# Grouped-key attention on one core: values issued four steps behind their scores in place of three

## The chip, the cores and the metric

One core of one Trainium2 chip runs the whole program. The metric is the device time of one execution in microseconds (us); of several executions the median is given. The engines are named as in the profile: PE (matmul), PEld (its weight loads), DVE (vector), ACT (scalar), POOL (GpSimd) and SP (which only issues DMAs here). Each runs its own instructions in order and waits for the others on semaphores.

## What is computed

The program chains a first block (pool mixer, windowed attention, feed-forward with convolution) and a second block of two attention layers, with 1024 tokens and 256 context tokens of width 1024, all in float32. The change lies in the first of the two layers, where 16 query heads of width 64 share 4 key heads:

```
def gqa_attend(q, k, v):
    s = jnp.einsum('bqhgd,bkhd->bhgqk', q, k).astype(jnp.float32) * (GQA_HEAD_DIM ** -0.5)
    p = jax.nn.softmax(s, axis=-1).astype(v.dtype)
    return jnp.einsum('bhgqk,bkhd->bqhgd', p, v)
...
    k_all = jnp.concatenate([kc, k], axis=1)
    v_all = jnp.concatenate([vc, v], axis=1)
    o = sweep_query_blocks(lambda qb: gqa_attend(qb, k_all, v_all), q).reshape(B, S, GQA_WIDTH)
    y = (o * jax.nn.silu(g)) @ p["w_out"]
...
        oc = gqa_attend(qc, kc, vc).reshape(B, L, GQA_WIDTH)
```

The 1024 tokens attend to all 1280 keys; the 256 context tokens attend to the 256 context keys. The second layer (called mla in the code) uses the same class of the kernel with other sizes.

## The kernel before, in words

The class `Attention` runs one attention layer for all 16 heads. The 1280 queries stand in three chunks (`CHUNKS_ALL`: 512, 512 and the 256 of the context), the keys in tiles of 128. A **step** is one key tile against one chunk: ten for each of the first two chunks, two for the context chunk, 22 a head. Two heads (44 steps, `self.SB`) make one turn of an 8-turn loop, in which the steps of one turn and the last values of the turn before are laid into each other. Operands are split into a high and a low part in a reduced float32 form so that products keep their precision.

What a step k does, engine by engine:

- PE, `scores` (L2253, L2254): two matmuls into one of two PSUM banks (`self.S[k % 2]`). It waits until exp of step k-2 has read the bank.
- ACT, `probs`: exp from PSUM into `gqa_pf` (L2314), then a copy into the reduced form, the high half `gqa_ph` (L2320). There are four buffers each of `PF`, `PH` and `PL`; exp of k waits for the low part of k-4, the high half of k waits for the values of k-4. Between the two ACT instructions, at certain steps, stand the two ACT instructions of the reciprocal (`rden`, L2330, L2332: a logarithm of the row of denominators, then exp of its negative).
- POOL, in some steps DVE (`low`, L2366): the low part `gqa_pl` = pf - ph. DVE takes it in steps 7, 9, 13 and 19 of a head (`dve_lo`), one step later in its own order.
- PE, `values` (L2268 to L2270): three matmuls that add into the output bank of the chunk. It waits for the low part. The output of the context chunk is kept in the bank `BC`.

Beside these, the row maxima of a later head or chunk are prepared. The table `self.plan` says at which step of a head PE passes over the keys (`maxima`, L2223, into the one PSUM area `PMX`: steps 0, 2 and 4 for chunk 1, step 6 for the context chunk, 10, 12, 14 and 16 for chunk 0 of the next head, 18 for its chunk 1); DVE reduces it (L2388), and after the last pass of a chunk DVE builds a diagonal matrix (L2396); in steps 8, 11 and 20 PE spreads it over the partitions (`bcast`, L2234, into `BC`), and ACT copies one row into the query tile (`row`, L2307). A pass of maxima waits for the reduction of the pass before. A broadcast waits for the diagonal, for the row before it, and for the multiply by the reciprocal (`self.norm`) of all chunks of the heads before, since that reads `BC`.

When a chunk has its last values, ACT makes the reciprocal and DVE runs `final`: a multiply of the output with the reciprocal into `gqa_t` (L2407, signals `norm`), and a multiply with the gate into `MIX` (L2412).

The order of the instructions of every engine is fixed when the program is built. In its step k, PE issues maxima and broadcasts of step k, then `scores(k)`, then `values(k - LAG)`. ACT runs the reciprocal of a chunk `LAG + 1` steps behind the chunk's last step (context chunk: `LAG + 2`). DVE issues the reductions and diagonals of step k, the low part of step k-1 where it is its own, and then the `final` that is due, by `self.lags`:

```
self.lags = (self.LAG + 4, self.LAG + 4, 0) if self.mla else (self.LAG + 5, self.LAG + 2, self.LAG + 3)
...
self.run(pe, first_steps, lambda i, k: values(i, k - self.LAG), self.LAG)
...
lags, lag = (self.LAG + 1, self.LAG + 1, self.LAG + 2), self.LAG + (1 if self.mla else 2)
```

The last steps of the chunks are 9, 19 and 21 of a head.

Of the kernel before, what the change touches and what calls it, by code (L numbers as in the profile page):

```python
# [104 lines left out]
def mixed_program(nc, A, out):  # L105

    ctx = ExitStack()
    with ctx:

        def sem(name):  # L110
            return ctx.enter_context(nc.semaphore(name))
# [4 lines left out]
        class Scope:  # L116


            def __init__(self):
                self.stack = ExitStack()  # L120
# [1880 lines left out]
        def head_buffers(name, scope, q, layout, nq, side="left"):  # L2001

            return ([scope.sb(f"{name}_k{a}{q}", [P, N], R32, side) for a in range(2)],
                    [scope.sb(f"{name}_q{a}{q}", [P, nq], R32, side) for a in range(2)],
                    [scope.sb(f"{name}_v{a}{q}", [P, N // P, P], R32, side) for a in range(2)])
# [5 lines left out]
        class Attention:  # L2011
# [4 lines left out]

            LAG = 3

            def __init__(self, name, scope, chunks, keys, scale, layout, mix, first, first_maxima):
                self.name, self.chunks, self.keys, self.scale, self.mix = name, chunks, keys, scale, mix
                self.mla = layout == "mla"
                self.row = 96 if self.mla else 64

                self.K, self.Q, self.V = zip(first, head_buffers(name, scope, 1, layout, chunks[-1][0] + chunks[-1][1]))
                self.G = scope.sb(f"{name}_gate", [P, chunks[-1][0] + chunks[-1][1]])
                self.PF = [scope.sb(f"{name}_pf{b}", [P, C]) for b in range(4)]
                self.PH = [scope.sb(f"{name}_ph{b}", [P, C], R32) for b in range(4)]
                self.PL = [scope.sb(f"{name}_pl{b}", [P, C], R32) for b in range(4)]  # L2030
                self.D = [first_maxima[0], scope.sb(f"{name}_d1", [P, 4, P], R32)]
                self.M = first_maxima[1]
                self.dim = 96 if self.mla else 64
                self.nq = chunks[-1][0] + chunks[-1][1]
                self.load_inc = 16 * (4 if self.mla else 6)

                self.const_n = 32 + 3 + (32 if self.mla else 0)
                self.v_and_const = [sem(f"{name}_v_and_const{q}") for q in range(2)]
                self.RD = scope.sb(f"{name}_rd", [64, C])
                self.T = scope.sb(f"{name}_t", [P, C])  # L2040
                self.loaded = [sem(f"{name}_loaded{q}") for q in range(2)]
                self.gate_loaded = sem(f"{name}_gate_loaded")
                (self.max, self.red, self.diag, self.bcast, self.row_done, self.scores, self.exp, self.hi,
                 self.lo_pool, self.lo_dve, self.pv, self.rden, self.norm, self.fin) = [sem(f"{name}_{x}") for x in (
                     "max", "red", "diag", "bcast", "row", "scores", "exp", "hi", "lo_pool", "lo_dve", "pv",
                     "rden", "norm", "fin")]
                self.S = [PB[0], PB[1]]
                self.BC = PB[2]
                self.FREE = self.BC if self.mla else PMX[:, 0:C]
                self.O = [PD[0], PD[1], self.BC]  # L2050

                self.steps = [(q, c, t, x == 0, x == len(keys[c]) - 1) for q in range(2) for c in range(len(chunks))
                              for x, t in enumerate(keys[c])]
                self.SB = len(self.steps)
                self.NC = len(chunks)

                if self.mla:
                    plan = [(2 * t, "max", (0, 1), t) for t in range(4)] + [(8, "bcast", (0, 1), 0)]  # L2060
                    plan += [(10 + 2 * t, "max", (1, 0), t) for t in range(4)] + [(18, "bcast", (1, 0), 0)]
                    self.ahead = [(0, t) for t in range(4)]
                else:
                    plan = [(2 * t - 2, "max", (0, 1), t) for t in range(1, 4)] + [(6, "max", (0, 2), 0)]
                    plan += [(8, "bcast", (0, 1), 0), (11, "bcast", (0, 2), 0)]
                    plan += [(10 + 2 * t, "max", (1, 0), t) for t in range(4)]
                    plan += [(18, "max", (1, 1), 0), (20, "bcast", (1, 0), 0)]
                    self.ahead = [(0, t) for t in range(4)] + [(1, 0)]
                self.plan = plan
                self.NT = sum(1 for p in plan if p[1] == "max")  # L2070
                self.fin_all = HEADS * self.NC + CR_FIN2
                self.norm_all = HEADS * self.NC + CR_N

                self.dve_lo = lambda k: k % (self.SB // 2) in ((3, 8, 13, 18) if self.mla else (7, 9, 13, 19))
                self.lags = (self.LAG + 4, self.LAG + 4, 0) if self.mla else (self.LAG + 5, self.LAG + 2, self.LAG + 3)
                self.n_dve = sum(1 for k in range(self.SB) if self.dve_lo(k))
                self.n_pool = self.SB - self.n_dve
# [123 lines left out]
            def pe_begin(self, pe):  # L2201
# [25 lines left out]
                def bcast(i, c, g):  # L2227
                    n = self.chunks[c][1]
                    pe.wait_ge(self.diag, i * (2 * NC) + (g + 1))

                    pe.wait_ge(self.row_done, i * (2 * NC) + (g + CR_ROW2))
                    if NC == 3:
                        pe.wait_ge(self.norm, i * (2 * NC) + ((g - 1) // NC * NC + CR_N))
                    pe.matmul(self.BC[:, 0:n], ones[:, :], self.D[g % 2][:, 0:n // P, :], start=True, stop=True)\  # L2234
                      .then_inc(self.bcast, 1)
# [21 lines left out]
                def values(i, k):  # L2257
                    q, c, t, first, last_ = self.steps[k]
                    n = self.chunks[c][1]
                    self.wait_lo(pe, i, k)  # L2260
                    if first and c == 0:
                        pe.wait_ge(self.v_and_const[q], i * 32 + self.const_n)
                    if first:

                        pe.wait_ge(self.norm, i * (2 * NC) + (q * NC + c - NC + CR_N + 1))
                    o = self.O[c][:, 0:n]
                    ph, pl = self.PH[k % 4][:, 0:n], self.PL[k % 4][:, 0:n]
                    pe.matmul(o, self.V[q][0][:, t, :], ph, start=first, stop=False)  # L2268
                    pe.matmul(o, self.V[q][1][:, t, :], ph, start=False, stop=False)  # L2269
                    pe.matmul(o, self.V[q][0][:, t, :], pl, start=False, stop=last_).then_inc(self.pv, 1)  # L2270
# [4 lines left out]
                def step(i, k, last):  # L2275
                    for kind, q, c, t, g, tile, over in self.tasks(k, last):
                        if kind == "max":
                            maxima(i, q, c, t, tile, c == 0 and t == 0, i + 1 if over else i)
                        else:
                            bcast(i, c, g)  # L2280
                    scores(i, k)

                def rest(bank_free):
                    def first_steps(i, k, last):
                        if isinstance(i, int) and i == 0 and k < 2:
                            bank_free(k)
                        step(i, k, last)
                    self.run(pe, first_steps, lambda i, k: values(i, k - self.LAG), self.LAG)
                return ahead, lambda: bcast(0, 0, 0), rest
# [7 lines left out]
            def act_begin(self, act):  # L2297
# [41 lines left out]

                lags, lag = (self.LAG + 1, self.LAG + 1, self.LAG + 2), self.LAG + (1 if self.mla else 2)  # L2340

# [1213 lines left out]
```

## Time and profile before

| what | us |
| --- | --- |
| median of 3 runs | 3461.96 (3459.22 to 3461.97) |
| the profiled execution | 3465.23 |
| its span, first to last instruction | 3463.3 |
| busy in the span: PE, DVE, ACT, POOL | 3330.5, 2261.4, 1769.3, 1538.4 |

The profile is of one execution. A start and a duration are in us from the start of the span. A duration of a matmul includes the time in the pipeline, so that consecutive matmuls overlap: two matmuls of 512 columns start 0.23 us apart and are shown with 0.39 us each. What a matmul costs is therefore read from start to start. PE appears as busy for nearly the whole program, in this stage too.

### The profile page before, as it was taken

How to read it: one execution, taken by the hardware profiler on the slowest of the kernel's cores; microseconds unless marked ns; L12 is line 12 of the kernel's file. 1: busy time of each engine (PE TensorE's matmuls, PEld its weight loads, DVE VectorE, ACT ScalarE, POOL GpSimd, SP SyncE). 2: the span in 40 equal slices, each digit the busy share in tenths (PEclk: the TensorE clock that was granted, in tenths of full speed). 3: DMA queues.
4: the chain of work that ended last, by engine and by line, in shares of the span. 5: the costliest groups of instructions: out<-in, count | busy, mean ns of one | idle time of the engine just before them, and what ended most of it. 6: DMA issues, size and time to landing. Idle time of an engine off the chain costs nothing.

```text
span 3463.3 us, 47931 instructions
## 1 busy us (share of the span) xinstructions
PE 3330.5 (96%) x14993; PEld 2652.2 (77%) x14993; DVE 2261.4 (65%) x2647; ACT 1769.3 (51%) x3039; POOL 1538.4 (44%) x962
## 2 busy tenths in 40 slices
PE   7999999999999999999999999999998989999999
PEld 5778878778888888778777777778765668888877
DVE  6674878677576665638537777777558875555551
ACT  3343878332010101334339999971455558888880
POOL 3403444544444445410037777767220026666662
PEclk9999999999999999999999999999999999999999
DMA  2134232411213121123344434413255344232312
GB/s 103 49 115 136 55 86 52 154 53 55 85 47 99 49 85 58 61 70 118 117 116 99 96 82 95 106 49 109 100 198 157 124 120 129 58 81 67 70 36 80
DMA packets 196088, 313.56 MB, mean 91 GB/s; under 512 B 100928, under 2 KB 111680, under 8 KB 195968
## 3 DMA queue, kind: packets, MB, share of 16 engines
q1 hardware_dynamic: 195968, 312.01, 31.3%
q8 instruction: 70, 1.15, 0.1%
q14 instruction: 50, 0.41, 0.0%
HBM read 234.02 MB, written 77.92 MB: 90 GB/s over the span
## 4 chain that ended last, share of the span: by engine, by line
PE 66%; POOL 10%; issue 9%; DVE 9%; ACT 4%; DMA 1%; SPq 0%; POOLq 0%; DVEq 0%; ACTq 0%
PE PBX L283 11%; PE PBX L285 10%; PE PBX L284 10%; POOL gqa_pl L2366 8%; PE PMX L283 4%; PE PMX L284 4%; PE PMX L285 4%; PE PMX L2223 2%; PE PD L2268 2%; PE PD L2269 2%; PE PD L2270 2%; PE PBX L2250 2%; PE PBX L2249 2%; PE PBX L2251 2%; PE PD L1013 2%
## 5 line engine op out<-in xcount | busy, mean ns | idle before, releaser
L216 POOL TENSOR_TENSOR w_hi<-w_stage,zero 128x1024 fp32r<-128x1024 f32 (+2 forms) x116 | 223.6, 1927 | 1173.6 <-PE PBX L285 875.7
L2366 POOL TENSOR_TENSOR gqa_pl<-gqa_pf,gqa_ph 128x512 fp32r<-128x512 f32 (+1 forms) x288 | 381.6, 1342 | 146.8 <-ACT gqa_ph L2320 145.0
L2366 POOL TENSOR_TENSOR mla_pl<-mla_pf,mla_ph 128x512 fp32r<-128x512 f32 x256 | 341.9, 1341 | 207.8 <-ACT mla_ph L2320 202.3
L2388 DVE TENSOR_REDUCE mla_m<-PMX 128x1 f32<-128x1280 f32 x128 | 190.9, 1491 | 173.2 <-PE PMX L2223 173.0
L2388 DVE TENSOR_REDUCE gqa_m<-PMX 128x1 f32<-128x1280 f32 x144 | 201.6, 1400 | 150.5 <-PE PMX L2223 149.8
L218 POOL TENSOR_TENSOR w_lo<-w_stage,w_hi 128x1024 fp32r<-128x1024 f32 (+2 forms) x116 | 293.9, 2534 | 9.1
L1904 ACT ACTIVATE conv_in<-PBX 128x512 f32<-128x512 f32 x66 | 39.4, 599 | 478.9 <-PE PBX L285 474.9
L2314 ACT ACTIVATE mla_pf<-PBX 128x512 f32<-128x512 f32 x320 | 190.1, 594 | 82.1 <-PE PBX L2251 67.8
L2320 ACT ACTIVATE gqa_ph<-gqa_pf 128x512 fp32r<-128x512 f32 (+1 forms) x352 | 214.9, 611 | 12.4 <-PE PD L2270 0.4
L2314 ACT ACTIVATE gqa_pf<-PBX 128x512 f32<-128x512 f32 (+1 forms) x352 | 200.6, 570 | 31.0 <-PE PBX L2254 20.1
L283 PE MATMUL PBX<-ffn_hi,w_hi 128*128 128x512 f32 x528 | 207.2, 392 | 4.5 <-DVE ffn_lo L710 4.5
L2320 ACT ACTIVATE mla_ph<-mla_pf 128x512 fp32r<-128x512 f32 x320 | 201.8, 631 | 11.4
L285 PE MATMUL PBX<-ffn_hi,w_lo 128*128 128x512 f32 x528 | 206.2, 390 | 0.0
L284 PE MATMUL PBX<-ffn_lo,w_hi 128*128 128x512 f32 x528 | 206.1, 390 | 0.0
L1933 DVE SCALAR_TENSOR_TENSOR conv_out<-conv_in,VEC,conv_out 128x1024 f32<-128x1024 f32 x88 | 188.0, 2136 | 12.8 <-DVE conv_out L1933 0.6
L283 PE MATMUL PBX<-l_hi,w_hi 128*128 128x512 f32 (+1 forms) x400 | 158.6, 396 | 8.1 <-DVE l_lo L710 6.2
L478 DVE SCALAR_TENSOR_TENSOR PMX<-mod_w,cond_s 128x1024 f32<-128x1024 f32 x96 | 159.6, 1663 | 5.7 <-DVE PMX L478 0.6
L1929 DVE TENSOR_SCALAR conv_out<-conv_in,VEC 128x1024 f32<-128x1024 f32 x44 | 73.1, 1662 | 134.5 <-ACT conv_in L1904 133.8
L1620 POOL TENSOR_TENSOR swa_pl<-swa_pf,swa_ph 128x512 fp32r<-128x512 f32 x64 | 81.5, 1273 | 157.4 <-ACT swa_ph L1545 157.1
L2268 PE MATMUL PD<-gqa_ph,gqa_v 128*128 128x512 f32 x320 | 138.2, 432 | 7.9 <-POOL gqa_pl L2366 4.6
L285 PE MATMUL PBX<-l_hi,w_lo 128*128 128x512 f32 (+1 forms) x400 | 145.0, 362 | 0.0
L284 PE MATMUL PBX<-l_lo,w_hi 128*128 128x512 f32 (+1 forms) x400 | 144.7, 362 | 0.0
(526 smaller groups left out, 9961.5 us busy)
## 6 DMA issues: line engine op xcount, KB each, us to landing
mod_w<-in_w_mod SPq DMA_DIRECT2D x48, 512.0 KB, 3.5
w_stage<-in_w_up SPq DMA_DIRECT2D x44, 512.0 KB, 3.5
w_stage<-in_w_go SPq DMA_DIRECT2D x24, 512.0 KB, 3.7
gqa_k<-kh_d SPq DMA_DIRECT2D x32, 320.0 KB, 5.1
gqa_q<-qh_d SPq DMA_DIRECT2D x32, 320.0 KB, 6.8
w_stage<-in_w_down SPq DMA_DIRECT2D x24, 384.0 KB, 3.1
qh_d<-heads_qh SPq DMA_DIRECT2D x32, 256.0 KB, 2.0
ql_d<-heads_ql SPq DMA_DIRECT2D x32, 256.0 KB, 2.3
```

What stands on the lines that cost most here:

```text
L216: pool.tensor_tensor(w_hi[s][:, 0:st.cols], w_stage[s][:, 0:st.cols], z, ALU.add).then_inc(w_hi_done, 1)
L218: pool.tensor_tensor(w_lo[s][:, 0:st.cols], w_stage[s][:, 0:st.cols], w_hi[s][:, 0:st.cols].bitcast(F32), ALU.subtract).then_inc(w_split, 1)
L283: pe.matmul(ps, wh, xh, start=first, stop=False)
L284: pe.matmul(ps, wh, xl, start=False, stop=False)
L285: return pe.matmul(ps, wl, xh, start=False, stop=last)
L478: dve.scalar_tensor_tensor(out=PMX[:, C:3 * C], in0=bufs[s], scalar=1.0, in1=conds[j], op0=ALU.mult, op1=ALU.mult, accum_out=MOD[:, bass.d ...
L1933: dve.scalar_tensor_tensor(out=y, in0=CU[s][:, j:j + S], scalar=w(j), in1=y, op0=ALU.mult, op1=ALU.add).then_inc(conv_step, 1)
L2268: pe.matmul(o, self.V[q][0][:, t, :], ph, start=first, stop=False)
L2314: act.activation(self.PF[k % 4][:, 0:n], self.S[k % 2][:, 0:n], ACT.Exp, scale=self.scale)\
L2320: act.activation(self.PH[k % 4][:, 0:n], self.PF[k % 4][:, 0:n], ACT.Copy).then_inc(self.hi, 1)
L2366: eng.tensor_tensor(self.PL[k % 4][:, 0:n], self.PF[k % 4][:, 0:n], self.PH[k % 4][:, 0:n].bitcast(F32), ALU.subtract).then_inc(self.lo_dv ...
L2388: dve.tensor_reduce(self.M[g % 2][:, t:t + n], PMX[:, 0:n * w].rearrange("p (n w) -> p n w", n=n), AX.X, ALU.max, negate=True).then_inc(se ...
```

## The change

The constant `LAG` of the class, 3, becomes a value of each object: 3 for the mla layer, 4 for the grouped-key layer. Everything that is counted from it follows: `values` of step k stand behind `scores` of step k+4; the reciprocals of the chunks move from steps 13, 1 and 4 to 14, 2 and 5; the finals on DVE from 17, 2 and 5 to 18, 3 and 6 (the later numbers of chunks 1 and 2 are steps of the next head). The number of buffers (four), the plan of the maxima, the steps whose low part DVE makes, and the number of instructions are the same. The unrolled start of the loop of each engine is one step longer.

```
-            LAG = 3
...
                 self.dim = 96 if self.mla else 64
+
+                self.LAG = 3 if self.mla else 4
```

## Rows read from the trace of the kernel before

**Rows 1.** Stretches: busy us (instructions) of each engine, granted clock, DMA share, GB/s

```profile
1786.00:2303.00 517.00, 504.54 (x2206) 388.70 (x2206) 382.98 (x346) 469.71 (x846) 383.57 (x290) 1.00 0.41 86
...
1916.53:1948.55 32.02, 31.56 (x142) 24.45 (x141) 24.24 (x22) 29.37 (x53) 24.06 (x19) 1.00 0.47 102
1948.55:1980.60 32.05, 31.60 (x142) 24.43 (x141) 24.77 (x22) 29.39 (x53) 23.86 (x19) 1.00 0.40 82
```

**Rows 2.** Timeline of PE, a middle head: start us, us, line, tiles

```profile
1927.97 0.39 PE L2253 MATMUL PBX<-gqa_q,gqa_k 128*128 128x512 f32 x1
...
1948.55 0.40 PE L2253 MATMUL PBX<-gqa_q,gqa_k 128*128 128x512 f32 x1
...
1949.71 0.40 PE L2253 MATMUL PBX<-gqa_q,gqa_k 128*128 128x512 f32 x1
```

**Rows 3.** Page, chain that ended last: shares of the span by line

```profile
PE PBX L283 11%; PE PBX L285 10%; PE PBX L284 10%; POOL gqa_pl L2366 8%; PE PMX L283 4%; PE PMX L284 4%; PE PMX L285 4%; PE PMX L2223 2%; PE PD L2268 2%; PE PD L2269 2%; PE PD L2270 2%; PE PBX L2250 2%; PE PBX L2249 2%; PE PBX L2251 2%; PE PD L1013 2%
```

**Rows 4.** Waits from 1832.35 to 2280.6: waiter <- awaited, us, times, longest

```profile
PEld PD L2268 <- POOL gqa_pl L2366: 37.2, 91, 0.7
...
ACT gqa_pf L2314 <- PE PBX L2254: 13.4, 26, 1.0
...
ACT gqa_ph L2320 <- PE PD L2270: 0.4, 1, 0.4
```

**Rows 5.** Timeline of PE, steps 5 to 8 of a head

```profile
1955.34 0.39 PE L2254 MATMUL PBX<-gqa_q,gqa_k 65*128 65x512 f32 x1
1955.99 0.50 PE L2268 MATMUL PD<-gqa_ph,gqa_v 128*128 128x512 f32 x1 [0.26 <-POOL gqa_pl L2366]
1956.32 0.39 PE L2269 MATMUL PD<-gqa_ph,gqa_v 128*128 128x512 f32 x1
...
1956.79 0.39 PE L2223 MATMUL PMX<-gqa_k,gqa_q 128*128 128x256 f32 x2
...
1959.74 0.39 PE L2234 MATMUL PBX<-gqa_d,ones 128*128 128x512 f32 x1
```

**Rows 6.** Timeline of ACT, steps 0 and 1 of the same head

```profile
1949.29 0.60 ACT L2314 ACTIVATE gqa_pf<-PBX 128x512 f32<-128x512 f32 x1 [1.03 <-PE PBX L2254]
...
1951.08 0.60 ACT L2330 ACTIVATE gqa_rd<-PD 64x512 f32<-64x512 f32 x1
1951.71 0.63 ACT L2332 ACTIVATE gqa_rd<-gqa_rd 64x512 f32<-64x512 f32 x1
```

**Rows 7.** Timeline of POOL, the same head

```profile
1952.94 8.82 POOL L2366 TENSOR_TENSOR gqa_pl<-gqa_pf,gqa_ph 128x512 fp32r<-128x512 f32 x6 [1.02 <-ACT gqa_ph L2320]
```

**Rows 8.** Timeline of DVE, steps 2 to 6 of the same head

```profile
1952.72 0.68 DVE L2407 TENSOR_TENSOR gqa_t<-PD,gqa_rd 64x512 f32<-64x512 f32 x1
1953.54 1.24 DVE L2412 TENSOR_TENSOR MIX<-gqa_t,gqa_gate 64x512 f32 x1
1954.71 1.47 DVE L2388 TENSOR_REDUCE gqa_m<-PMX 128x1 f32<-128x1280 f32 x1
1956.22 1.52 DVE L2396 TENSOR_TENSOR gqa_d<-ident_f,gqa_m 128x512 fp32r<-128x512 f32 x1
1957.66 0.41 DVE L2407 TENSOR_TENSOR gqa_t<-PBX,gqa_rd 64x256 f32<-64x256 f32 x1
...
1959.09 0.67 DVE L2388 TENSOR_REDUCE gqa_m<-PMX 128x2 f32<-128x512 f32 x1
1959.80 0.81 DVE L2396 TENSOR_TENSOR gqa_d<-ident_f,gqa_m 128x256 fp32r<-128x256 f32 x1
```

**Rows 9.** Timeline of DVE, the first head

```profile
1791.68 0.99 DVE L2396 TENSOR_TENSOR gqa_d<-ident_f,gqa_m 128x512 fp32r<-128x512 f32 x1
```

**Rows 10.** Timeline of PE, first head and last head

```profile
1801.06 0.85 PE L2223 MATMUL PMX<-gqa_k,gqa_q 128*128 128x512 f32 x3 [3.50 <-DMA gqa_v<-vl_d]
...
2280.07 0.40 PE L2234 MATMUL PBX<-gqa_d,ones 128*128 128x512 f32 x1
```

**Rows 11.** Timeline of ACT, last head, the row copy of step 8

```profile
2281.39 0.59 ACT L2307 ACTIVATE gqa_q<-PBX 1x512 fp32r<-1x512 f32 x1
```

## What the change is predicted to do, before it ran

> **What bounds the kernel now.** I read the stage windows first. The grouped-key stage runs from about 1786 to 2302 us, 517 us of the 3463.3 us span, at a full granted clock [rows 1]; the stage with the other layout keeps its lag of three and everything outside the stage issues the same instructions, so only these 517 us can change. Inside it one head of 22 steps repeats: two heads in a row took 32.02 and 32.05 us, with PE busy 31.6, ACT 29.4, DVE 24.2 to 24.8 and POOL 24.0 [rows 1]. PE looks full, but the page says a busy PE need not be at its peak, so I went by start-to-start times. Write S(k) for the two score matmuls of step k, V(k) for the three value matmuls, M for a maxima pass, B for a broadcast. A step without M lasts 1.16 us from S to S [rows 2]: five matmuls at 0.233. So S is 0.47, V 0.70, M 0.57 to 0.58, the small M of step 6 0.23, B 0.23, and a step of the context chunk (256 queries) 0.24 and 0.35.
>
> The chain that ended last gives POOL's low parts 8% of the span [rows 3], and the waits of the middle of the stage put 37.2 us on value matmuls that wait for POOL [rows 4]. That counts from the end of a weight load, so it overstates. By start-to-start times six V in a head start late: V(2) starts 0.65 us after its step's second score matmul in place of 0.235, and its own second matmul follows after 0.33 in place of 0.235, a loss of 0.51 us [rows 5]. The other five lose 0.41, 0.31, 0.31, 0.29 and 0.25 by the same reading; together 2.1 us a head. Without them PE's head is 32.0 - 2.1 = 29.9 us. The prize is at most 16 x 2.1 = 34 us.
>
> **The edits.** Every count is the same: no instruction, DMA or buffer is added. Three things move by one step.
>
> (a) V(k) is issued after S(k+4), not S(k+3). A high half follows its S by about 1.4 us, by 2.6 where a reciprocal (two ACT ops; its first begins 0.61 after its exp, its second 0.63 later [rows 6]) lies between; then the low part takes 1.29 to 1.47 (8.82 us for six [rows 7]). The late V above are those where this exceeds three steps. A further step gives 1.16 to 1.74 us, over twice the largest delay. I take all six delays as gone: -2.1 us a head. The lower bound is 0 (POOL is at 24.0 of 32, so it is no bound by itself).
>
> (b) ACT's high half of k needs V(k-4) out of the buffer. Before, V(k-4) was issued ahead of S(k); now it is behind it. S(k) starts at 0, exp(k) at 0.74 (S(0) at 1948.55, exp at 1949.29 [rows 2, 6]) and the high half would start at 1.37; V(k-4) starts at 0.47, its last matmul ends 0.87 later, about 0.1 goes to the hand-over, so 1.44. Cost: 0.07 us where ACT follows PE at once, nothing where it lags. ACT's own pair is 1.15 us and PE's step 1.16, so the 0.07 is paid once as an offset, not per step. Between 0 and 20 x 0.07 = 1.4 us a head; I take 0.
>
> (c) The ends of chunks. The reciprocals move from steps 13, 1 and 4 to 14, 2 and 5, and DVE's two multiplies of a chunk ("final") from 17, 2 and 5 to 18, 3 and 6. DVE executes in order, a step's maxima first, then its final. So the final of chunk 1 used to stand behind the reduction of step 2, and now stands alone in step 3, in front of the reduction of step 4; the final of the context chunk used to stand in front of step 6's reduction and diagonal, and now stands behind both. Two PE instructions wait for this: M of step 6 needs the reduction of step 4 (one PSUM area), and B of step 8 needs the multiply of the context chunk's final (it reads the bank that B writes). Before, B(8) came at 1959.74 and that multiply began at 1957.66 and took 0.41: 1.67 us of slack [rows 5, 8]. M(6) at 1956.79 came 0.6 after the reduction of step 4 (1954.71 + 1.47) [rows 5, 8].
>
> The new order, in us from S(0), by those durations: S(0) 0, V(18) 0.47, S(1) 1.16, V(19) 1.63, M(2) 2.33, S(2) 2.90, exp(2) 3.64 (ACT is free by 3.15). Reciprocal 4.25 and 4.88, done 5.51. Final of chunk 1 begins at 5.55. Then DVE runs without a gap, start to start as in [rows 8]: multiply 0.82, MIX multiply 1.17, reduction of step 4 1.51, diagonal 1.44, small reduction 0.71, small diagonal 0.75 to 0.81, then the context multiply 0.41: it ends at 12.36. M(6) can start at 9.1, where PE arrives at about 7.7; B(8) starts at 12.4, where PE could be at 10.1 by its own work. So 2.3 us of waiting per head stands in place of 1.2 us of late V ahead of B(8) before. After B(8): restart 0.34 (as at 1955.99 to 1956.32 [rows 5]), then S(8) to the next S(0). Before this was 1948.55 - 1927.97 = 20.58 us with 0.91 of late V in it, so 19.67 pure (the two starts are in [rows 2]). The head becomes 12.41 + 0.34 + 19.67 = 32.4 us, against 32.03. I followed ACT and POOL through these 20 us: exp(k-2) is out 0.3 us or more ahead of S(k), and the tightest low part (17) ends 0.5 us before its V.
>
> The other half of the heads shows the same DVE order; with the shorter ops that the trace also has for the same work (diagonal 0.99 in the first head [rows 9]) the chain is 0.3 shorter to 0.3 longer: head 32.1 to 32.75.
>
> The Trainium skill bears here, "SBUF — State Buffer", section "SBUF: two separate sides": it says that a VectorE op with two SBUF inputs and a GpSimd op that reads SBUF take a shared port pair as an exclusive lock, and that whoever comes second blocks for the other's whole instruction. This trace shows a milder thing: POOL's ops went from 1.29 to 1.47 and the diagonal next to them took 1.52 against 0.99 [rows 7 to 9]. By the rule at its full size the three ops of the new chain with two SBUF inputs could each wait out a POOL op of 1.29 us, 3.9 us a head in place of the 0.7 that the rows hold; it would end at the second rival or above.
>
> **The sum.** First head: PE waits for the second head's values from DRAM until 1801.06 whatever came before [rows 10]; its last two late V go, -0.6. Then 14 head to head periods at +0.38: +5.3. B(8) of the last head sits 12.41 - 11.19 = +1.2 later from its S(0). Behind it no maxima are left and ACT sets the pace; its row copy came 1.32 us after B(8) (2281.39 - 2280.07 [rows 10, 11]) and now can follow after 0.5: -0.85. Sum -0.6 + 5.3 + 1.2 - 0.85 = +5.1 us. The profiled execution took 3465.23 (span 3463.3), 3.3 above the median 3461.96; the sum gives 3470.3 for such an execution and 3467.1 for the median. With the heads at 32.1 to 32.75 this case spans 3463 to 3472.
>
> **Rivals.**
> 1. Faster: the final chain is short or begins early enough that M(6) and B(8) do not wait. Then only ACT's pace is left: exp(3), exp(6) and the like hold S by some 0.7 us a head, 29.9 + 0.7 = 30.6, so 14 x -1.4 - 0.6 - 0.85 = -21: 3441. For it: the late V are real and 34 us are there. Against: M(2) holds exp(2), and the seven DVE ops are counted in rows. It would need B(8) by 10.6, 1.8 us less than counted. Chance 0.13.
> 2. Slower by more: MIX, diagonal and small diagonal each wait out part of a POOL op that now stands elsewhere. By half of 1.29 us for each of the three, 1.9 us, less the 0.7 already in the rows taken: +1.2 a head, 14 x 1.2 + 5.1 = +22: 3484. It decides once the context multiply ends after 12.9 us from S(0). For it: POOL is busy without a break from low(2) on. Against: it was so in the rows I used. Chance 0.13.
> 3. No change: ACT, at 29.4 of 32 us, sets the pace under (b), loses what V gains, and the period stays within 0.1 us: 3462. Speaks for it: 92% busy. Speaks against: ACT waited 13.4 us for scores in the middle stretch, and only 0.4 for values [rows 4]. Chance 0.12.
>
> **Chances.** Forecast 0.62, rivals 0.13, 0.13, 0.12. A measurement of this kernel can tell some 0.2%, 6.9 us, from no change. Of the forecast's case about 0.4 of the width lies above +6.9 in view of errors of 0.1 us in each of seven ops, and a little below zero: slower 0.25 + 0.13 = 0.38; faster 0.13; same 0.37 + 0.12 = 0.49. The range leaves out most of rival 1 and half of rival 2: 3453 to 3480; the likeliest case's own is 3460 to 3474.
>
> **What would show it.** In the changed trace: (a) right if no value matmul waits for POOL in a middle head; (b) right if the high half waits for values by 0.1 us or less; (c) right if DVE runs seven ops without a gap between 5.5 and 12.4 us from S(0), if M(6) starts 0.05 to 0.1 after the reduction of step 4, and B(8) right behind the multiply of the context chunk, with PE gaps of about 1.4 and 0.8 us ahead of them, and S(0) to S(0) at 32.4. It is wrong if B(8) starts ahead of 11 us from S(0), if the reciprocal of chunk 1 runs at another step, or if POOL still holds values.

## The result and the profile after

The change made the kernel slower: 3473.56 us (median of 6 runs, 3471.29 to 3476.04) against 3461.26 (6 runs, 3459.22 to 3464.47), a ratio of 1.0032 with a 95% interval of 1.0021 to 1.0042. Measured once more in another series it was 1.004 (1.0027 to 1.0052). Forecast was 3467.1 with a range of 3453 to 3480: the sign of the forecast's sum (+5.1 us) and the mechanism came out, but the size was under half of the 12.3 us measured. The profiled execution has a span of 3474.1 us, 10.8 above that before.

The chain that ended last, from the page of the changed kernel, answers to [rows 3]: POOL's low parts, 8% before, are no longer among its listed lines, and POOL's part of the whole chain fell from 10% to 1%, while DVE's rose from 9% to 11%. First the shares by engine before the change, then those after it by engine and by line:

```profile
PE 66%; POOL 10%; issue 9%; DVE 9%; ACT 4%; DMA 1%; SPq 0%; POOLq 0%; DVEq 0%; ACTq 0%
...
PE 76%; DVE 11%; issue 6%; ACT 4%; POOL 1%; DMA 1%; SPq 0%; DVEq 0%; ACTq 0%; POOLq 0%
PE PBX L283 11%; PE PBX L285 10%; PE PBX L284 10%; PE PMX L283 4%; PE PMX L284 4%; PE PMX L285 4%; PE PMX L2224 4%; PE PD L2269 4%; PE PD L2270 4%; PE PD L2271 4%; PE PBX L2251 2%; PE PBX L2250 2%; PE PBX L2252 2%; PE PD L1013 2%; PE PBX L2255 2%
```

The waits of the changed kernel in the middle of the stage (1832.35 to 2290) answer to [rows 4]; columns: waiter <- awaited, us in all, times, longest.

```profile
PEld PMX L2224 <- DVE gqa_m L2389: 24.5, 14, 1.8
PEld PBX L2235 <- DVE gqa_t L2408: 9.7, 11, 0.9
PEld PBX L2254 <- ACT gqa_pf L2315: 6.8, 14, 0.5
...
ACT gqa_ph L2321 <- PE PD L2271: 0.9, 2, 0.7
...
DVE gqa_t L2408 <- ACT gqa_rd L2333: 13.9, 14, 1.1
```

(All lines of the class are one further down than before.) No value matmul waits for POOL. In place of the 37.2 us of [rows 4] PE waits for two things of DVE, once a head each: the small maxima pass of step 6 for a reduction, and the broadcast of step 8 for the context chunk's multiply. The last line is where the DVE chain starts: DVE stands idle there until the reciprocal is ready.

The timeline of DVE in one middle head, from the pass of step 2 to the low part of step 7 (S(0) of this head starts at 1949.65), answers to [rows 8]:

```profile
1952.78 1.49 DVE L2389 TENSOR_REDUCE gqa_m<-PMX 128x1 f32<-128x1280 f32 x1 [1.44 <-PE PMX L2224]
1955.32 0.68 DVE L2408 TENSOR_TENSOR gqa_t<-PD,gqa_rd 64x512 f32<-64x512 f32 x1 [1.05 <-ACT gqa_rd L2333]
1956.15 1.47 DVE L2413 TENSOR_TENSOR MIX<-gqa_t,gqa_gate 64x512 f32 x1
1957.56 1.47 DVE L2389 TENSOR_REDUCE gqa_m<-PMX 128x1 f32<-128x1280 f32 x1
1959.06 1.49 DVE L2397 TENSOR_TENSOR gqa_d<-ident_f,gqa_m 128x512 fp32r<-128x512 f32 x1
1960.47 0.68 DVE L2389 TENSOR_REDUCE gqa_m<-PMX 128x2 f32<-128x512 f32 x1
1961.19 0.80 DVE L2397 TENSOR_TENSOR gqa_d<-ident_f,gqa_m 128x256 fp32r<-128x256 f32 x1
1961.91 0.41 DVE L2408 TENSOR_TENSOR gqa_t<-PBX,gqa_rd 64x256 f32<-64x256 f32 x1
```

and the timeline of PE in the same head answers to [rows 2, 5]:

```profile
1949.65 0.40 PE L2254 MATMUL PBX<-gqa_q,gqa_k 128*128 128x512 f32 x1
...
1959.08 0.50 PE L2224 MATMUL PMX<-gqa_k,gqa_q 128*128 128x256 f32 x2 [1.25 <-DVE gqa_m L2389]
...
1962.37 0.50 PE L2235 MATMUL PBX<-gqa_d,ones 128*128 128x512 f32 x1 [0.44 <-DVE gqa_t L2408]
1962.70 0.39 PE L2254 MATMUL PBX<-gqa_q,gqa_k 128*128 128x512 f32 x1
...
1982.47 0.40 PE L2254 MATMUL PBX<-gqa_q,gqa_k 128*128 128x512 f32 x1
```

The reader is to see that DVE runs seven ops without a gap from 1955.32 to 1962.32, that PE's small pass starts 0.05 us after the reduction (1957.56 + 1.47 = 1959.03), that the broadcast starts 0.05 us after the multiply (1961.91 + 0.41 = 1962.32), and that a head lasts 1982.47 - 1949.65 = 32.82 us. Taken from the small pass of one head to that of the next, alternate heads of the changed kernel take 32.7 and 32.9 us; before they took 32.0 and 32.1. One head, from 2188.89 on, took 33.49. In it the granted clock of PE fell to half, 1.2 GHz in place of 2.4, right after PE's usual wait for the small pass, and the matmuls start 0.43 us apart in place of 0.23:

```profile
2189.00:2193.00 4.00, 4.00 (x12) 3.21 (x13) 3.36 (x5) 2.41 (x5) 2.90 (x3) 0.57 0.94 140
```

The third number from the end is the granted clock. PE had waited as long in the other heads without such a fall; why it came here isn't shown.

### The profile page after: what moved, and what is told of

It reads as the page before. It is cut to its first block, busy times and chain, and to the rows that moved or that the text cites. A ratio compares the mean times of both kernels' runs of the same rounds, so it can differ in the third digit from the quotient of the medians.

```text
span 3474.1 us, 47931 instructions
## 1 busy us (share of the span) xinstructions
PE 3320.1 (96%) x14993; PEld 2654.2 (76%) x14993; DVE 2256.6 (65%) x2647; ACT 1771.0 (51%) x3039; POOL 1539.6 (44%) x962
## 3 DMA queue, kind: packets, MB, share of 16 engines
q8 instruction: 70, 1.15, 0.1%
## 4 chain that ended last, share of the span: by engine, by line
PE 76%; DVE 11%; issue 6%; ACT 4%; POOL 1%; DMA 1%; SPq 0%; DVEq 0%; ACTq 0%; POOLq 0%
PE PBX L283 11%; PE PBX L285 10%; PE PBX L284 10%; PE PMX L283 4%; PE PMX L284 4%; PE PMX L285 4%; PE PMX L2224 4%; PE PD L2269 4%; PE PD L2270 4%; PE PD L2271 4%; PE PBX L2251 2%; PE PBX L2250 2%; PE PBX L2252 2%; PE PD L1013 2%; PE PBX L2255 2%
## 5 line engine op out<-in xcount | busy, mean ns | idle before, releaser
L283 PE MATMUL PBX<-h_hi,w_hi 128*128 128x512 f32 x336 | 138.8, 413 | 2.1 <-issue 1.1
```

Of the source, the lines that this page charges most:

```text
L283: pe.matmul(ps, wh, xh, start=first, stop=False)
```

## The experiments

All start from the changed kernel; a number after `else` is for the grouped-key layer. "Head" is the mean time from the small maxima pass of one head to that of the next, over 13 to 15 heads of the profiled execution. A head with a stretch at half clock is left out (one in the change, one with the reciprocals late). Waits "in the middle of the stage" are those from 1832.35 to 2270, which is 20 us less than in the list above; the change itself has 22.8 us for the small pass and 9.7 for the broadcast in it.

**Values four behind, ends where they were.**

```
-self.lags = ... else (self.LAG + 5, self.LAG + 2, self.LAG + 3)
+self.lags = ... else (8, 5, 6)
...
-lags, lag = (self.LAG + 1, self.LAG + 1, self.LAG + 2), self.LAG + (1 if self.mla else 2)
+lags, lag = (4, 4, 5), (4 if self.mla else 5)
```

> Only the values move to four steps behind; reciprocals stay at steps 13, 1 and 4 of a head and finals on DVE at 17, 2 and 5, as before the change. Theory (the chain of finals on DVE costs the time): the chain starts 1 us earlier and the context chunk's multiply stands ahead of the small reduction, B(8) waits for nothing, M(6) for about 0.6 us. Head 30.7 us from S(0) to S(0) against 32.0 before and 32.8 after; some 20 us faster than before, 3441. Rival (the coupling of the high half to the values, part b, costs the time): as slow as the change, 3473.

Measured: 3444.0 us, 0.9943 (0.993 to 0.9955) of before; head 30.64 us. The waits of PE in the middle of the stage (counted, as in [rows 4], from the end of a weight load):

```profile
PEld PBX L2254 <- ACT gqa_pf L2315: 6.0, 20, 0.7
PEld PMX L2224 <- DVE gqa_m L2389: 5.6, 14, 0.5
PEld PD L2269 <- POOL gqa_pl L2367: 1.8, 6, 0.3
```

The wait for POOL fell from 35.6 us before the change (37.2 up to 2280.6 [rows 4]) to 1.8 and nothing of that size came in its place. Moving the values alone is worth -1.4 us a head, so the loss of the change lies wholly in its other half, the ends. The rival that the coupling of the high half costs the time has fallen for a lag of four.

**Values three behind, ends as in the change.**

```
-self.LAG = 3 if self.mla else 4
+self.LAG = 3
...
-self.lags = ... else (self.LAG + 5, self.LAG + 2, self.LAG + 3)
+self.lags = ... else (9, 6, 7)
...
-lags, lag = (self.LAG + 1, self.LAG + 1, self.LAG + 2), self.LAG + (1 if self.mla else 2)
+lags, lag = ((4, 4, 5) if self.mla else (5, 5, 6)), (4 if self.mla else 6)
```

> Values stay three steps behind; reciprocals and finals move to the places they have in the change (14, 2, 5 and 18, 3, 6). Theory: B(8) at 12.7 us from S(0) as in the change, and the late values after B(8), 0.9 us a head, are still there: head 33.7, 14 x 1.65 = +23 us on before, 3484. Rival (values and high half): as before, 3461.

Measured: 3489.04 us, 1.0075 (1.0061 to 1.0088); head 33.77 us. Both kinds of wait stand side by side:

```profile
PEld PD L2269 <- POOL gqa_pl L2367: 25.6, 52, 1.3
PEld PMX L2224 <- DVE gqa_m L2389: 19.3, 13, 1.5
PEld PBX L2235 <- DVE gqa_t L2408: 10.8, 12, 0.9
```

So the parts don't add from the kernel before: the ends alone cost +1.75 us a head, the values alone bring -1.4, together they give +0.8 and not +0.35. Late values ahead of B(8) are hidden under the wait at B(8); taking them away there brings nothing once that wait exists. What the values still bring is 33.77 - 32.82 = 0.95 us a head, close to the 0.91 us of late values that the prediction had counted behind B(8).

**Which of the two ends: finals late, or reciprocals late.** Two kernels, each the change with one of them put back.

```
-lags, lag = (self.LAG + 1, self.LAG + 1, self.LAG + 2), self.LAG + (1 if self.mla else 2)
+lags, lag = (4, 4, 5), (4 if self.mla else 5)
```

> The change with its reciprocals back at 13, 1 and 4; finals on DVE stay at 18, 3 and 6. Theory: the multiply of chunk 1 can begin at 4.65 us from S(0), right behind the reduction of step 2, in place of 5.67; the rest of the DVE chain is the same, 7.1 us, so B(8) at 11.8 and a head of 31.9 us: 3460, 13 us below the change. Rival: as the change, 3473.

```
-self.lags = ... else (self.LAG + 5, self.LAG + 2, self.LAG + 3)
+self.lags = ... else (8, 5, 6)
```

> The change with its finals on DVE back at 17, 2 and 5; reciprocals stay at 14, 2 and 5. Theory: the multiply of chunk 1 still begins at 5.6, so M(6) starts at 9.4 as in the change, but the context chunk's multiply stands ahead of the small reduction and B(8) comes when PE arrives, at 12.1. Head 32.1 to 32.2 us: 3463, 10 us below the change. Rival: as the change, 3473.

Measured: finals late 3447.35 us, 0.9954 (0.9942 to 0.9967), head 31.15; reciprocals late 3465.16 us, 1.0001 (0.9992 to 1.001), head 32.15. The second came as worked out. The first came 13 us below what was expected, and its DVE timeline shows where most of that arose (S(0) of this head starts at 1971.93):

```profile
1976.57 0.68 DVE L2408 TENSOR_TENSOR gqa_t<-PD,gqa_rd 64x512 f32<-64x512 f32 x1
1977.40 0.82 DVE L2413 TENSOR_TENSOR MIX<-gqa_t,gqa_gate 64x512 f32 x1
1978.25 1.49 DVE L2389 TENSOR_REDUCE gqa_m<-PMX 128x1 f32<-128x1280 f32 x1
1979.88 1.29 DVE L2397 TENSOR_TENSOR gqa_d<-ident_f,gqa_m 128x512 fp32r<-128x512 f32 x1
```

The multiply begins 4.64 us after S(0), as expected (4.65). But the MIX multiply takes 0.82 us and not 1.47; the whole chain is 6.5 us long and not 7.1, so B(8) comes at 1983.11, 11.2 us after S(0). POOL is at work in both cases. What differs is how much of POOL's op is left when the MIX multiply begins. Here are POOL's op under way with late finals (first line), and that in the change with the one after it:

```profile
1976.38 1.29 POOL L2367 TENSOR_TENSOR gqa_pl<-gqa_pf,gqa_ph 128x512 fp32r<-128x512 f32 x1 [1.00 <-ACT gqa_ph L2321]
...
1955.80 1.28 POOL L2367 TENSOR_TENSOR gqa_pl<-gqa_pf,gqa_ph 128x512 fp32r<-128x512 f32 x1 [1.45 <-ACT gqa_ph L2321]
1957.09 1.68 POOL L2367 TENSOR_TENSOR gqa_pl<-gqa_pf,gqa_ph 128x512 fp32r<-128x512 f32 x1
```

With late finals the POOL op ends 0.27 us after the multiply began (1977.67 - 1977.40), in the change 0.93 after it (1957.08 - 1956.15); in both, the multiply ends 0.55 us after the POOL op. A late reciprocal thus costs twice: its own 1 us, and 0.65 us since the MIX multiply then begins early in a POOL op and no longer near its end. The 0.6 us a head are some 9 of the 13 us.

The two ends have a wait each. Reciprocals late alone keep the whole wait of the small pass (22.8 us in the middle of the stage, as in the change) and free the broadcast (0 against 9.7 us). Finals late alone keep the wait of the broadcast (9.3) and leave 5.4 at the small pass:

```profile
PEld PBX L2235 <- DVE gqa_t L2408: 9.3, 12, 0.8
PEld PMX L2224 <- DVE gqa_m L2389: 5.4, 14, 0.5
```

Over the values alone (30.64) late finals cost 0.5 us a head, late reciprocals 1.5, both together 2.2.

**How much of the DVE chain is POOL's doing.** In steps 2 to 6 POOL writes zeros in place of the low part, all but one column, and so reads next to nothing; the values of those steps lack their low part.

```
-if not self.dve_lo(k):
+if not self.dve_lo(k) and not self.mla and 2 <= k % 22 <= 6:
+    pool.wait_ge(self.hi, i * self.SB + (k + 1))
+    pool.tensor_tensor(self.PL[k % 4][:, 0:1], self.PF[k % 4][:, 0:1],
+                       self.PH[k % 4][:, 0:1].bitcast(F32), ALU.subtract)
+    pool.memset(self.PL[k % 4][:, 1:C].bitcast(F32), 0.0).then_inc(self.lo_pool, 1)
+elif not self.dve_lo(k):
     self.low(pool, i, k)
```

> The change, but in steps 2 to 6 of each head POOL fills the low part with zero (one column is still computed, the rest is a memset that reads nothing), so that the low parts of these steps are left out of the values. It asks how much of the DVE chain is POOL's doing. Theory (POOL's reads stretch the MIX multiply and the two diagonals): MIX begins the reduction 0.85 after it in place of 1.4, the diagonal takes about 1.0 and the small one 0.47; chain 1.2 to 1.5 us shorter, B(8) at 11.4, head 31.6: 3457. Rival (the ops take this long by themselves): as the change, 3473.

Measured: 3451.91 us, 0.9977 (0.9968 to 0.9986) of before and so 21 us below the change; head 31.25 us. The chain on DVE, same ops as in the change (their lines stand five further down; S(0) of this head starts at 1942.39):

```profile
1948.06 0.68 DVE L2413 TENSOR_TENSOR gqa_t<-PD,gqa_rd 64x512 f32<-64x512 f32 x1 [1.06 <-ACT gqa_rd L2333]
1948.89 0.69 DVE L2418 TENSOR_TENSOR MIX<-gqa_t,gqa_gate 64x512 f32 x1
1949.50 1.48 DVE L2394 TENSOR_REDUCE gqa_m<-PMX 128x1 f32<-128x1280 f32 x1
1951.01 0.69 DVE L2402 TENSOR_TENSOR gqa_d<-ident_f,gqa_m 128x512 fp32r<-128x512 f32 x1
1951.63 0.68 DVE L2394 TENSOR_REDUCE gqa_m<-PMX 128x2 f32<-128x512 f32 x1
1952.34 0.43 DVE L2402 TENSOR_TENSOR gqa_d<-ident_f,gqa_m 128x256 fp32r<-128x256 f32 x1
1952.68 0.41 DVE L2413 TENSOR_TENSOR gqa_t<-PBX,gqa_rd 64x256 f32<-64x256 f32 x1
```

It lasts 5.0 us where the change needs 7.0. Three ops shrink, those that read two tiles from SBUF: MIX 1.47 to 0.69, the diagonal 1.49 to 0.69, the small one 0.80 to 0.43. The reductions and the multiplies, which read PSUM, keep their 1.48, 0.68 and 0.41. The chain begins 5.67 us after S(0), as in the change; M(6) then comes at 8.64 in place of 9.43 and B(8) at 11.3 in place of 12.7. That is worth 1.57 us a head, more than the change lost against the kernel before (0.8) and less than the ends cost (2.2): with this chain B(8) waits for nothing, but the small pass still does (12.5 us in the middle of the stage). POOL is also done sooner in these steps (0.65 us in place of 1.29), which is a second difference; no value matmul of the change waited for POOL, so I put the gain down to the chain, which is argued and not shown apart.

**One step further.** Values five behind, reciprocals as in the change, finals as before it; against the kernel with late reciprocals only the values move (`self.lags`, `lags` and `lag` are written out so that the ends stay as there).

```
-self.LAG = 3 if self.mla else 4
+self.LAG = 3 if self.mla else 5
```

> Values five steps behind with the same four buffers, reciprocals at 14, 2 and 5 (they need the values), finals on DVE at 17, 2 and 5: the fourth experiment with one more step between scores and values, so that the high half of k now stands behind the scores of k+1 as well. It prices the coupling of part b. Theory (the coupling is nearly free): at most one plain pair of steps in 2.66 us where PE takes 2.32 to 2.9, that is up to 1 us a head: 3465 to 3480. Rival (the coupling is what costs): every plain step 1.33 us in place of 1.16, 3 us a head, 3510 or more.

Measured: 3549.86 us, 1.0258 (1.0244 to 1.0272); head 37.5 us, 5.3 more than with four. The theory's part in this, that the coupling is nearly free, fell; it holds for four only. The waits of ACT and PE:

```profile
PEld PBX L2254 <- ACT gqa_pf L2315: 64.3, 104, 1.5
...
ACT gqa_ph L2321 <- PE PD L2271: 92.0, 152, 2.2
```

With a lag of five and four buffers the high half of k waits until PE has gone through the scores of k+1 and then the values of k-4, so ACT can no longer fall behind PE and catch up. My bound (2.66 us for a pair of steps) had only exp and high half in it. What it left out were ACT's other works, whose starts lie 1.15, 1.15 and 0.75 us (reciprocals) and 0.72, 0.72 and 0.5 us (rows) further than without them, 5.0 us a head. That sum is close to the 5.3 measured, and scores do wait behind such places, but that each of them goes to PE in full is argued from the sum and not shown by itself.

**Both attention layers, values alone.** The first experiment with a lag of four in the mla layer too.

```
-self.LAG = 3 if self.mla else 4
+self.LAG = 4
...
+self.lags = (7, 7, 0) if self.mla else (8, 5, 6)
...
+lags, lag = (4, 4, 5), (4 if self.mla else 5)
```

> The first experiment (values four steps behind, ends where they were) in both attention layers. Theory (only late values can be won): in the mla stage before the change PE waits for POOL's low parts 0.3 us in all, so there is nothing to win: as the first experiment, 3441 to 3446. Rival (a larger lag helps by itself): another 10 us or more.

Measured: 3444.27 us, 0.9959 (0.9945 to 0.9972), the same as the first experiment within the intervals. Where no values come late (PE waited 0.3 us in all for POOL's low parts in that stage before the change) nothing was won.

**What is left in the best version.** The first experiment, with the small maxima pass one step later; beside it the first experiment and the change once more.

```
-[(6, "max", (0, 2), 0)]
+[(7, "max", (0, 2), 0)]
```

> The first experiment with the small maxima pass of the context chunk in step 7 in place of 6. In the first experiment it is the only PE instruction that still waits for DVE (0.4 us a head). If PE sets the pace there, a head loses 0.3 to 0.4 us: 30.3, 5 us less than the first experiment, 3438. If ACT does (its rows stand without a gap from step 0 on in the first experiment), nothing: 3443.

> The first experiment once more, unchanged, beside the last one on the same chip: 0.994 of before, 3443.

> The change itself once more, on the same chip as the two others: 1.003 of before, 3473.

Measured side by side: small pass later 3443.96 us, 0.9951 (0.9938 to 0.9964); first experiment again 3441.74, 0.9947 (0.9934 to 0.996); the change again 3473.41, 1.004 (1.0027 to 1.0052). The wait for DVE is gone from PE's list and nothing was won. PE now waits for exp (6.6 us) and hardly for anything else. The 0.4 us a head that the expectation began with was counted from a weight load; start to start the small pass was only 0.1 us late (1.8 us in 14 heads), and with the pass in step 7 the scores behind it start late instead (2.6 us in 14 heads). The first experiment is the version that beats both kernels, by some 19 us against before and 31 against the change.

## Why the prediction was right and where it was off

**(a) Late values.** Right. PE's wait for POOL is gone (the list above), and alone this is worth 1.4 us a head. The 2.1 us of late V counted in the kernel before are not all won even without the ends; the first rival had counted 30.6 us for a head without the DVE chain, and the experiment gave 30.64.

**(b) High half behind the values.** Right for a lag of four. The high half waited for values twice in 14 heads, 0.68 and 0.27 us; both lie in the one stretch at half clock (at 2191.66 and 2193.38), so at full clock it did not wait at all. With the values alone it waited six times in the middle of the stage, 1.4 us in all, 0.3 at most. The third rival (ACT loses what V gains) fell with the first experiment.

**(c) The ends.** The mechanism is the one forecast, each link at its place; the rise of a head came out at twice the forecast, 0.8 us in place of 0.4:

| from S(0), us | forecast | measured |
| --- | --- | --- |
| final of chunk 1 begins | 5.55 | 5.67 |
| small pass M(6) | 9.1 | 9.43 |
| context multiply ends | 12.36 | 12.67 |
| B(8) | 12.41 | 12.72 |
| S(8) to the next S(0) | 19.67 | 19.77 |
| head | 32.4 | 32.82 |

The term that was mis-sized is the MIX multiply. I took its spacing in [rows 8], 1.17 us, where in the changed kernel the next op starts 1.41 after it. In the rows the multiply began at 1953.54, and the POOL op under way (the first of the six of [rows 7], 1.29 us long by itself) had 0.7 us to go; in the changed kernel the one under way has 0.93 to go. With 0.12 us at the start and 0.1 after B(8), less 0.06 in the other ops, that makes 0.4 us a head. So the head of 32.82 lies just outside the 32.1 to 32.75 given for this case, and the median just above its 3472.

I had put a longer MIX multiply as the second rival, at half a POOL op for each of three ops. It came at one op, and small: the change stands between the forecast's own case and that rival. The context multiply ended at 12.67, short of the 12.9 from which that rival was to decide. Of the two waits of PE the first came as forecast (1.4 us ahead of M(6), though PE got there 8.02 us after S(0) and not 7.7), the second at 0.6 in place of 0.8.

**The sum around it.** The span grew by 10.8 us where +5.1 was the sum. Fourteen heads with 0.4 more make 5.6 us of the 5.7 that are missing, but that this fits so closely is luck, for other terms were off too and largely cancel. The stretch at half clock added 0.8. The first head's wait for the DRAM load, which I took to end at 1801.06 "whatever came before", ended at 1799.44, 1.6 us earlier, and in a second profile of the same changed kernel at 1796.11: it differs from one execution to the next, and is no constant. B(8) of the last head is at 2291.33 against 2280.07 [rows 10], +11.26. From it to the last value matmul it is 2311.71 - 2291.33 = 20.4 us against 21.3 before, -0.9 where -0.85 was forecast.

**POOL's ops beside the chain.** The rule of the Trainium skill ("SBUF — State Buffer", "SBUF: two separate sides"), that a VectorE op with two SBUF inputs and a GpSimd op that reads SBUF hold a shared port pair as an exclusive lock, names the right three ops: exactly those shrank when POOL read next to nothing, and none of the others. The trace agrees with the lock too, and my reading of it in the prediction, "a milder thing", was wrong. The second comer waits for what is left of the op under way, and that was 0.93 us for MIX, 0.94 for the diagonal and 0.51 for the small one in the head above, after which the ops end 0.55, 0.55 and 0.28 us later. My 3.9 us a head stood for three waits of a whole POOL op, which would need each op to begin just behind the start of one. The 0.99 of [rows 9], which I compared with, had such a wait in it as well (the POOL op under way ended at 1792.12, the diagonal at 1792.67). So the length of the chain depends on where in a POOL op each of the three begins, and a later start must be followed through POOL's ops as well as through DVE's.

**Chances.** Slower had 0.38, no change 0.49. The threshold of 6.9 us lay 1.8 us above my sum, and an error of 0.13 us in one head was enough to cross it. With a term repeated 14 times, and seven ops in it, more of the forecast's case should have stood above the line.

## What to carry to other kernels

A lag constant often moves more than the thing it is named for: here it moved the values, which was worth 19 us, and with them the reciprocals and the finals on an in-order engine, which cost 31. Give each its own constant, and look for each moved instruction at what it now stands in front of. When a wait is taken out, find the next instruction in the loop that waits for another engine; waits ahead of it only become its slack. With n buffers the lag could be n, as long as the writer of the buffer still had room to fall behind: with four buffers here a lag of four left 1.4 us of such waiting in the whole middle of the stage, and at five the head went from 32.15 to 37.5 us. And where a short op has to wait for what is left of a longer one on another engine, as MIX did for POOL's, a forecast needs to say where in the longer op it begins.

## What the runs showed of the hardware

- A DVE op on two SBUF tiles that begins while POOL works on a low part ends 0.55 us after that POOL op (0.28 with 256 columns), however long it has to wait. In the kernel before this holds for all 106 such ops from 1832 to 2265, in the changed one for 84 of 90. In the other six, DVE's low part had its usual 0.68 us and POOL's op took 2.35. The DVE ops so took 0.70 to 1.70 us where they take 0.69 alone. An op that reads PSUM took the same in both (1.49, 0.68, 0.41).
- POOL's next op pays as well: in the run of five next to DVE's chain the ops took 1.28, 1.68, 1.28, 1.60 and 1.46 us, the longer ones being those that begin while a DVE op on two SBUF tiles is in progress.
- Next to a POOL memset, which only writes (0.53 us), the MIX multiply took its 0.69 us.
- From the end of a DVE op to the start of the PE matmul that waits for it went 0.05 us, both at the small pass and at the broadcast. The matmul behind such a wait then started 0.33 us later in place of 0.23.
